# The forget gates' 8-row products, one pair at a time between blocks of the value product

## The reference

```python
proj = xn @ w_in
fq, fk, fv, ff, gq, gk, gv, glr, gr = jnp.split(proj, _split_points(), axis=-1)
log_f = jax.nn.log_sigmoid((ff + fox_b_f).astype(jnp.float32))      # 8 heads
c = jnp.transpose(jnp.cumsum(log_f, axis=1), (0, 2, 1))
bias = c[:, :, start:end, None] - c[:, :, None, :end]               # forgetting attention
fox_out = fox_attention(fq, fk, fv, log_f)                          # softmax(q k + bias) v
gla_o = gla_chunked(gq, gk, gv, g_log)                              # 4 chunks of 64 tokens
gla_out = rms_norm_2(gla_o, gla_out_norm_g) * jax.nn.silu(gr)
return jnp.concatenate([fox_out, gla_out], axis=-1) @ w_out
```

## Time and profile before

| | |
|---|---|
| median of 3 runs | 1707.01 us (1703.74 to 1727.58) |
| the profiled execution | 1703.73 us, of these 1701.9 us from its first instruction to its last |
| TensorE busy | 1445.8 us, 85% of the span |
| DVE, ACT, POOL busy | 484.8, 349.6, 114.4 us |
| mean granted clock of TensorE | 0.975 of full speed |

### The profile page before, as it was taken

How to read it: one execution, slowest core, us unless ns; L and a number is a source line. 1 busy time by engine, 2 the same in 40 slices (tenths; PEclk the granted TensorE clock), 3 DMA queues, 4 the chain that set the end, 5 groups by cost and what they waited for, 6 DMA issues and landing times. The chain is left out here.

```text
span 1701.9 us, 17970 instructions
## 1 busy us (share of the span) xinstructions
PE 1445.8 (85%) x7722; PEld 786.3 (46%) x7722; DVE 484.8 (28%) x736; ACT 349.6 (21%) x523; POOL 114.4 (7%) x107
## 2 busy tenths in 40 slices
PE   5999978788887898699787877778777999999999
PEld 2744632232231232199421212222115767788997
DVE  1486530100110000166501001001004754435453
ACT  1122420010010000133200100000003634644432
POOL 0000000000000000100000000000003043440000
PEclk9999989999999999999899999999999989999999
DMA  9979969999999999994499999999999523425520
GB/s 374 405 320 413 374 253 422 416 414 421 417 421 422 413 421 421 406 372 166 179 422 421 422 422 422 422 421 422 422 422 355 188 100 130 145 105 193 198 100 25
DMA packets 110000, 561.83 MB, mean 330 GB/s; under 512 B 8516, under 2 KB 9908, under 8 KB 54126
## 3 DMA queue, kind: packets, MB, share of 16 engines
q1 hardware_dynamic: 105880, 551.76, 80.5%
q0 software_dynamic: 2208, 8.36, 1.4%
q10 hardware_dynamic: 1846, 0.75, 0.2%
HBM read 557.69 MB, written 3.16 MB: 330 GB/s over the span
## 5 line engine op out<-in xcount | busy, mean ns | idle before, releaser
L2178 PE MATMUL ps<-ring,scratch 128*32 128x512 f32 x3072 | 613.5, 599 | 138.8 <-DMA ring<-in_moe_w_down 64.0
L2178 PEld LDWEIGHTS ps<-ring,scratch 128*32 128x32 f32 x3072 | 153.7, 110 | 573.5 <-issue 336.5
L1918 PE MATMUL ps<-ring_parts,scratch_parts 128*128 128x512 f32 x656 | 185.8, 401 | 4.9 <-DVE xT_parts L1177 1.4
L1918 PE MATMUL ps<-scratch_parts,ring_parts 128*128 128x256 f32 x704 | 145.5, 282 | 0.0
L1918 PEld LDWEIGHTS ps<-ring_parts,scratch_parts 128*128 128x128 f32 x656 | 121.7, 188 | 35.3 <-issue 3.4
L600 ACT ACTIVATE ring_parts<-ring 128x2048 fp32r<-128x2048 f32 x56 | 106.2, 1918 | 92.2 <-PE ps L1918 86.0
L453 DVE TENSOR_TENSOR ring_parts<-ring,ring_parts 128x2048 fp32r<-128x2048 f32 x46 | 105.3, 2289 | 53.5 <-ACT ring_parts L600 52.2
L1918 PEld LDWEIGHTS ps<-scratch_parts,ring_parts 128*128 128x128 f32 x704 | 115.6, 190 | 0.3
L1507 DVE TENSOR_TENSOR scratch<-ps,gate_bc 128x512 f32<-128x512 f32 x16 | 11.1, 692 | 291.8 <-PE ps L2178 291.8
L1496 DVE TENSOR_TENSOR scratch<-scratch,ps 128x1024 f32<-128x1024 f32 x8 | 9.8, 1222 | 257.0 <-PE ps L2178 257.0
L1918 PE MATMUL ps<-xT_parts,ring_parts 128*128 128x256 f32 x288 | 81.1, 282 | 1.3 <-DVE xT_parts L1168 1.3
(11 more groups left out here) (392 smaller groups left out, 1507.4 us busy)
## 6 DMA issues: line engine op xcount, KB each, us to landing
ring<-in_moe_w_gate SPq DMA_DIRECT2D x64, 2048.0 KB, 30.0
ring<-in_moe_w_up SPq DMA_DIRECT2D x64, 2048.0 KB, 23.1
ring<-in_moe_w_down SPq DMA_DIRECT2D x64, 2048.0 KB, 32.8
ring<-in_ada_w SPq DMA_DIRECT2D x24, 2048.0 KB, 14.5
ring<-in_mlp_w SPq DMA_DIRECT2D x16, 2048.0 KB, 8.8
ring<-in_sc_w_in SPq DMA_DIRECT2D x6, 2048.0 KB, 21.4
ring<-in_w_in SPq DMA_DIRECT2D x6, 2048.0 KB, 18.5
ring<-in_xattn_wkv SPq DMA_DIRECT2D x4, 2048.0 KB, 33.5
```

Source lines behind the costliest of these rows:

```text
L1918: last = mm(out, lhs[x], rhs[y], start=start and n == 0, stop=stop and n == 2)
L2178: last = mm(ps[32 * j:32 * j + 32, banks[half], :], src[:, k, CAP * j:CAP * (j + 1)], w[:, j % (EG // RUN), F * (k % RUN) + col:F * (k % R ...
```

## The change

The 16 blocks of `w_fv` and the eight 8-row products are the same as before, and so is everything on the other engines. TensorE's order differs, and the place of two waits. One block of the first half of `w_fv` follows each pair of 8-row products; the wait for `values` therefore stands before the first of these blocks. The blocks 4 to 7 of the first half follow the four rounds of tile 0, the blocks 0 and 1 of the second half the first two rounds of tile 1, the last two rounds have none between them, and six blocks are left behind them. The wait for `nb`, 2, is moved ahead of tile 0's rounds.

```diff
             for j, b in enumerate(FT[0] + FT[1]):
                 ...
                 last.then_inc(sem("nb_ps"), 1)
+                if j == 0:
+                    pe.wait_ge(sem("values"), 4)
+                fv_block(0, j)
                 ...
             pe.wait_ge(sem("states"), 1)
+            pe.wait_ge(sem("nb"), 2)
             for hd in range(GLAH):
                 ...
                 last = gla_chunk(1, hd)
-                if hd == 0:
-                    pe.wait_ge(sem("values"), 4)
                 if hd < GLAH - 1:
-                    fv_block(0, hd)
+                    fv_block(0, 4 + hd)
             last.then_inc(sem("go_ps"), 1)
-            fv_block(0, GLAH - 1)
-            pe.wait_ge(sem("nb"), 2)
+            fv_block(0, 7).then_inc(sem("w_halves_used"), 1)
             for hd in range(GLAH):
                 ...
-                if hd < GLAH - 1:
-                    fv_block(0, 4 + hd)
+                if hd < 2:
+                    fv_block(1, hd)
             last.then_inc(sem("go_ps"), 1)
-            fv_block(0, 4 + GLAH - 1).then_inc(sem("w_halves_used"), 1)
-            for b in range(8):
+            for b in range(2, 8):
                 last = fv_block(1, b)
```

More of the change, by code:

```diff
@@ L2386, in _, with fv_block @@
             last.then_inc(sem("ccol_ps"), 1)
+            def fv_block(half, b):
+                return split_block(FIRST["w_fv"], half, b // 4, b % 4, x, FO[b // 4])
             for j, b in enumerate(FT[0] + FT[1]):
@@ L2404, in gla_chunk @@
                           state[64 * w:64 * w + 64, r, c - 1, :], start=False, stop=True)
-            i = FIRST["w_fv"]
-            def fv_block(half, b):
-                return split_block(i, half, b // 4, b % 4, x, FO[b // 4])
             pe.wait_ge(sem("states"), 1)
+            pe.wait_ge(sem("nb"), 2)
             for hd in range(GLAH):
```

## The result

| | median of 12 runs | lowest |
|---|---|---|
| before | 1705.95 us | 1703.15 us |
| changed | 1712.40 us | 1709.92 us |

The forecast was 1701, the range 1695 to 1710. What came is the third rival, to which I had given 0.10: the clock falls already among the first pairs, and stays down. (2 of the 12 executions before and 4 of the 12 of the changed kernel took some 22 us more than the median; none of these has a trace.)

The account below looks back on a forecast made before the run. TensorE alone was taken to bound the stretch, 13.6 us of it at half clock. Its 5.35 us gain, cut by a 1.1 us POOL wait, gave 4.2: 1703.7 - 4.2 = 1699.5, plus 1.7 for run spread, 1701 us; range 1695 to 1710.

Parts of the forecast that it names:

- the third rival: Clock falls already in the first pairs, returns only in tile 1: 5.3 us slower, 1710.7 us; chance 0.10.
- I take it that it stays up: TensorE's clock stays at 1.00 through the pairs and rounds, since blocks are 45% as in the forgetting attention.
- The other evidence against it: After the fall, blocks taking 1.58 of each 2.83 us round did not bring the clock back for four rounds.
- The sum of that rival: First pair to transposes at the low clock: transposes at 1405.2 instead of 1399.85 us, 5.3 slower.
- the three pairs: 8-row pairs at 0.50, each put between 0.89 and 1.78 us, the middle 1.3 taken: 3.9 us together.
- The sum for a clock that stays up: TensorE from first pair to transposes: own gain 5.35 us; with the wait for POOL, 4.2, so about 23.1 us.
- the forecast of 1.76: One cycle of lone block, pair and change over at full clock: 0.79 + 0.89 + 0.08 = 1.76 us.
- 1.1 forecast: Before the transposes, TensorE, ready at 1394.5, waits 1.1 us for POOL's `mix_rows`.
- A full-clock round of tile 0: Linear attention, tile 0: own products 0.70 and block 0.89, 1.59 us a round instead of 2.83 at 0.50.
- Each moves by the same 4.2: Behind the transposes, ACT's and DVE's steps leading into the forgetting attention each come 4.2 us earlier.
- The profile shows one execution only: Caveat: the median would be off if the stretch at 0.50 is not in each run of the kernel before.
- The new wait for `values`: After the first pair, TensorE waits for ACT's reads of the banks before the first block: costs 0.15 us.

Follow-up runs that it names:

- two_blocks_8rows: Changed kernel, still 8 rows, with two blocks behind each pair instead of one and tile 0's rounds bare: 1701.7 us against 1705.5 for the kernel before.
- rows128_after: Changed kernel with the gates' products contracting over 128 rows instead of 8, the added rows zeros: 1721.1 us against 1705.2 for the kernel before.
- blocks_first: Kernel before, but eight blocks follow the 8-row products in one row, then the linear attention without blocks: 1702.7 us against 1705.2.

## Why the prediction was wrong, step by step

- **"I take it that it stays up"** is the step that failed. It rested on one comparison: blocks were 45% of the forgetting attention, where the clock is 1.00, and would be 45% of the alternation. The remainder was treated as alike, though I had noted that it has 64 or 128 rows there and 8 here. The runs show that this was the point: 64 rows hold the clock even with no block between them, 32 do not, and 8-row products want two blocks to a pair instead of one.
- **The other evidence against it was read and set aside.** Blocks with narrow products between them did not bring the clock back for four rounds. In the changed kernel the pairs and lone blocks did not either. The fall within the pairs lasted through the rest of them, tile 0's four rounds and most of tile 1's first two. That is why the third rival's stretch is so long.
- **The sum of that rival** was 5.3 us, measured 6.5. The mis-sized term is the three pairs: 3.9 us in the sum, 1.05 + 2.00 + 2.00 = 5.05 in the trace. A pair at half clock takes more than my upper bound of 1.78. The wait for POOL, 0.41, was not in that sum; against this, the three blocks took 1.20 + 1.58 + 1.58 = 4.36 instead of 4.7, since the clock fell only within the first of them.
- **The sum for a clock that stays up** came out with 128 rows: 22.7 us measured and 23.1 forecast. For 8 rows it was too short: at full clock a pair between blocks takes 1.05, and two blocks behind it 1.59 (two_blocks_8rows), so with a lone block 1.05 + 1.59 - 0.70 = 1.94 to a cycle, where I had 1.76. With 128 rows a cycle is 0.86 + 0.70 = 1.56. That the forecast of 1.76 lies between them is luck. POOL's tile 1 starts right behind its tile 0 in this run and TensorE waits 0.88 us (1.1 forecast); line 1101 takes 3.26 us beside DVE again. A full-clock round of tile 0 is 0.37 + 0.36 + 0.91 = 1.64 us (1.59). In the changed kernel itself TensorE was so late that POOL's work cost it only 0.41 us.
- **"Each moves by the same 4.2"** failed in the changed order with 128 rows. The new wait for POOL adds idleness just ahead of the forgetting attention, and in each of four executions some 21 us were lost behind it until the waits were filled. I had priced the wait at its own length. With 8 rows and two blocks to a pair the same was lost in two executions of twelve.
- **"The profile shows one execution only"** did not matter for the stretch at 0.50: the order before, with 8 and with 32 rows, shows it in two traces, some 13.6 us long in both.

The new wait for `values`, which I charged with 0.15 us, was 0.03 in the chain.

## What to carry to other kernels

Read the granted clock beside each stretch in which TensorE is "busy", and look at what ran just ahead of a fall: here a few microseconds of products over 8 of 128 rows, which cost 6 us in all. If such a product picks or spreads a row, give it more rows of zeros (64 were enough here); it takes about the same time (3.65 us instead of 3.56) and needs no new order. And before a wait is accepted as short, look at what runs behind it: the forgetting attention kept the clock that it found, high or low, and behind two waits of about a microsecond it ran 21 us longer, in one kernel every time and in others now and then.

## What the runs showed of the hardware

- In the order before, with some 3.6 us of these products in a row, the clock falls with 8 and with 32 contraction rows and stays with 64 and with 128. The added rows are all zeros.
- The forgetting attention runs at either level: 1.00 in the traces of eight kernels, 0.50 for 47.7 us in those of rows128_after and two_blocks_8rows, all the work being the same. The linear attention's rounds of tile 0, with a block to each, stay at 0.50 when they start there and at 1.00 when they start there. Full blocks in a row brought the clock back after 3.4 us.
- A pair of 8-row products between blocks takes 1.05 us at 2.4 GHz and 2.00 at 1.2 GHz; with 128 rows a pair takes 0.86 at 2.4 GHz.
- Work whose result nobody reads was worth 21 us in one place: one product of 0.9 us ahead of each of two waits. Longer idleness in the same place (1.64 and 1.15 us in blocks_first) left the clock at 1.00 in that trace, so its length alone does not decide.
